# GDN entry of a hybrid decoder step on one NeuronCore: the first head's preparation interleaved with the decay chain, its weights divided by ScalarE and VectorE, the norm's high parts on ScalarE

## What is computed

```
h = x * rsqrt(mean(x*x) + eps) * w                # pre-norm, then
proj = h @ w_in                                   # GDN: q, k, v, z per head, and a, b (8 + 8 columns)
q, k, v = silu(causal_conv(qkv)); q, k = l2norm(q), l2norm(k)
beta = sigmoid(b);  g = -exp(A_log) * softplus(a + dt_bias);  G = cumsum(g) in each chunk
decay = exp(G_t - G_s);  M = I + strict_lower(beta * (k k^T) * decay)      # M is inverted by levels
A = (q k^T) * decay;  then the recurrence over chunks with M^-1, k, v and the state
```

## Time and profile before

| quantity | value |
|---|---|
| median of three runs | 1971.35 us |
| the profiled execution | 1978.76 us, its span 1976.5 us |
| TensorE busy | 92% of the span |
| VectorE / ScalarE / GpSimd busy | 57% / 27% / 25% |
| granted TensorE clock, mean | 0.951 |
| GDN entry, last tiles of U_AB to x2 of head 0 | 895 to 971.8 us of the span |

### The profile page before, as it was taken

One profiled execution on the slowest core, in us unless ns is written; L12 is line 12 of the kernel. 1 busy time (PEld: TensorE's weight loads), 2 busy tenths in 40 slices (PEclk: granted clock), 3 DMA queues, 4 the chain that ended last, 5 costly groups with the idle time before them and its releaser, 6 DMA issues.

```text
span 1976.5 us, 34445 instructions
## 1 busy us (share of the span) xinstructions
PE 1827.2 (92%) x13499; PEld 1743.0 (88%) x13499; DVE 1131.8 (57%) x1862; ACT 534.4 (27%) x981; POOL 499.1 (25%) x279
## 2 busy tenths in 40 slices
PE   3999999999999999997799999999989899999997
PEld 2888888888999999997788888888878799999996
DVE  5677777766625262676566666667653552525253
ACT  1444444443100000013243344344431300000011
POOL 1100000001556565662000000000000365655562
PEclk9989899989999999998798998999989899999997
DMA  5122222222232222331211211220112133222321
GB/s 173 46 63 67 63 68 73 65 76 78 75 86 86 86 85 86 92 77 45 55 35 36 65 47 30 56 67 21 45 52 69 51 90 86 86 85 85 88 82 45
DMA packets 257706, 136.76 MB, mean 69 GB/s; under 512 B 6730, under 2 KB 255908, under 8 KB 257636
## 3 DMA queue, kind: packets, MB, share of 16 engines
q1 hardware_dynamic: 219988, 115.08, 20.5%
q10 hardware_dynamic: 37648, 20.68, 3.6%
HBM read 123.75 MB, written 12.00 MB: 69 GB/s over the span
## 4 chain that ended last, share of the span: by engine, by line
PE 44%; DVE 5%; ACT 2%; issue 2%; DVEq 0%; ACTq 0%
PE pj L500 29%; PE rr L799 2%; PE rr L792 1%; PE rr L521 1%; PE rr L763 1%; PE rr L538 1%; DVE pr L1718 1%; PE rr L781 1%; PE rr L698 1%; PE rr L708 1%; DVE ol L1952 1%; DVE ws L1843 1%; PE rr L868 0%; PE rr L718 0%; PE rr L873 0%
## 5 line engine op out<-in xcount | busy, mean ns | idle before, releaser
L461 POOL TENSOR_SCALAR w_hi<-w_raw 128x1024 fp32r<-128x1024 f32 x137 | 145.2, 1060 | 1431.4 <-PE pj L500 1380.4
L500 PE MATMUL pj<-xh,w_hi 128*128 128x272 f32 x2064 | 468.1, 309 | 16.7 <-DVE xl L1452 7.7
L500 PE MATMUL pj<-xh,w_lo 128*128 128x272 f32 x2064 | 439.6, 295 | 0.0
L500 PE MATMUL pj<-xl,w_hi 128*128 128x272 f32 x2064 | 438.7, 295 | 0.0
L500 PEld LDWEIGHTS pj<-xh,w_hi 128*128 128x128 f32 x2064 | 335.5, 196 | 40.6 <-issue 19.8
L463 POOL TENSOR_TENSOR w_lo<-w_raw,w_hi 128x1024 fp32r<-128x1024 f32 x137 | 353.5, 2581 | 11.4
L500 PEld LDWEIGHTS pj<-xl,w_hi 128*128 128x128 f32 x2064 | 336.8, 196 | 0.0
L500 PEld LDWEIGHTS pj<-xh,w_lo 128*128 128x128 f32 x2064 | 335.9, 196 | 0.0
L500 PE MATMUL pj<-oh,w_hi 128*128 128x272 f32 x1248 | 264.9, 294 | 5.7 <-DVE w_lo L1497 3.1
L500 PE MATMUL pj<-oh,w_lo 128*128 128x272 f32 x1248 | 260.1, 290 | 0.0
L500 PE MATMUL pj<-ol,w_hi 128*128 128x272 f32 x1248 | 259.6, 290 | 0.0
(11 more groups left out here) (295 smaller groups left out, 2312.3 us busy)
## 6 DMA issues: line engine op xcount, KB each, us to landing
w_raw<-in_mlp_w_up_dram SPq DMA_DIRECT2D x64, 512.0 KB, 4.0
w_raw<-in_mlp_w_down_dram SPq DMA_DIRECT2D x64, 512.0 KB, 4.0
w_raw<-in_hgrn_w_in_dram SPq DMA_DIRECT2D x32, 512.0 KB, 4.1
w_raw<-in_gdn_w_in_dram SPq DMA_DIRECT2D x32, 512.0 KB, 4.2
out_dram<-S ACTq DMA_DIRECT2D x16, 512.0 KB, 3.4
w_raw<-in_hgrn_w_out_dram SPq DMA_DIRECT2D x9, 512.0 KB, 3.9
w_raw<-in_gdn_w_out_dram SPq DMA_DIRECT2D x9, 512.0 KB, 4.0
S<-in_state_hgrn_dram ACTq DMA_DIRECT2D x8, 512.0 KB, 4.1
```

Of the source, the lines that this page charges most:

```text
L461: nc.gpsimd.tensor_scalar(w_hi[:, s], w_raw[:, j], 1.0, 1.0, ALU.mult, ALU.mult).then_inc(hi_pool, 1)
L500: last = mm(pj[:, s, b, 0:HALF], w[:, s, k, :], v[:, k, b * HALF:(b + 1) * HALF], start=(k == 0 and a == 0), stop=(k == end - 1 and a == 2))
```

## The change

Four edits.

1. **The norm's high parts.** In n0 and n2 the product x*w into `xh` moves from VectorE (L1450) to ScalarE, an activation with the weight column as its scale, right after the square of the same k. VectorE's low part waits for it.
2. **Units 1 to 3 leave GpSimd.** `on_gpsimd` ends at U_GIN + 1. ScalarE's `high` of units 1, 2, 3 stands in `gdn_pre`; VectorE's `low` of 1 and 2 in `gdn_pre`, of 3 ahead of slot L3. `high` of 4 and 5 moves from behind the slots to behind L4 and L6, `low` of 4 and 5 to ahead of the evacuation of z and ahead of C0.
3. **Preparation inside the decay chain.** VectorE evacuates unit 0 and does slot L1 before the scan, and evacuates unit 1 at the end of the chain. The transposes of the history stand ahead of unit 0 on TensorE, and ScalarE does L1 and the first tap of k inside the chain. For head 0 the evacuations of v and z get places of their own (`evac2`, `evac3`). In all heads the copy `gnext` and the product `gsel` move from slot L1 to behind the convolution of k (L2). VectorE does `move` right behind `inverse`.
4. **All tiles of units 2 to 5 between the slots.** TensorE's counts are 4, 4, 6, 5, 5, 3, 2 ahead of L3, L4, L5, L6, C0, C2, C3, and 3 ahead of the first inverse: 32 tiles. Nothing stands between the first inverse and the recurrence.

```diff
 def on_gpsimd(u):
-    return u < 4 or U_MLP0 <= u < U_GIN + 4 or u >= U_MLP1
+    return u < 4 or U_MLP0 <= u < U_GIN + 1 or u >= U_MLP1
 # TensorE
 first_unit(U_AB, "n2")
-more = head_projections(U_GIN, 0)
-more(2 * KT)
+gdn_prepare("L1", 0)
+unit(U_GIN, 0, 0, xh, xl)
+unit(U_GIN, 0, 1, xh, xl)
 gdn_pre()
 pe.wait_ge(st["gp"][1].sem, st["gp"][1].after("cols", 0))
-for slot in GDN_SLOTS:
-    more(0 if slot == "L0" else 2)
+more = head_projections(U_GIN, 0, 2, 6)
+for slot, n in (("L3", 4), ("L4", 4), ("L5", 6), ("L6", 5), ("C0", 5), ("C2", 3), ("C3", 2)):
+    more(n)
     gdn_prepare(slot, 0)
+more(3)
 gdn_first_inverse(0, (st["ga"][1], "cout", 0))
-head_projections(U_GIN, 1, 0, 2)(2 * KT)
 # ScalarE, norm
     s.did(f(sq[:, k % 2], xT[:, k], ACT.Square), f"sq{k}")
+    if wcol is not None:
+        s.did(f(xh[:, k], xT[:, k], ACT.Copy, scale=vec[:, wcol + k:wcol + k + 1]), f"hi{k}")
 # ScalarE, gdn_pre
+high(0, U_GIN + 1)
+gdn_prepare("L1", 0)
 s.did(f(gsc[0:H, 2:3], gsc[0:H, 0:1], ACT.Exp), "A")
 ...
 s.did(f(gt4[32:64], B[32:64, 2], ACT.Exp), "be")
+high(0, U_GIN + 2)
+gdn_prepare("L2x", 0)
 ...
 s.did(f(gt4[96:96 + H], gt4[0:H], ACT.Exp), "eg")
+high(0, U_GIN + 3)
 sem_of(t, "cols", 0)
 # ScalarE, slots of head 0
+if slot == "L4":
+    high(0, U_GIN + 4)
+if slot == "L6":
+    high(0, U_GIN + 5)
 # VectorE, norm
-v.did(ts(xh[:, k], xT[:, k], w, None, ALU.mult), f"hi{k}")
-after(v, f"hi{k}", 0)
+after(s, f"hi{k}", 0)
 # VectorE, gdn_pre
 v.did(stt(... "neg")
+low(0, U_GIN + 1)
 ...
 v.did(ts(... "g2")
+gdn_prepare("evac0", 0)
+gdn_prepare("L1", 0)
 ...
 v.did(less_than_last(b[3][0:H], gt4[0:H]), "dl")
+low(0, U_GIN + 2)
+gdn_prepare("evac1", 0)
 # VectorE, slots of head 0
-for slot in GDN_SLOTS + ["inverse"]:
+for slot in ("L2", "L3", "L4", "evac2", "evac3", "L5", "L6", "C0", "C1", "C2", "C3", "inverse", "move"):
+    # low of unit 3 ahead of L3, of unit 4 ahead of evac3, of unit 5 ahead of C0
     gdn_prepare(slot, 0)
-low(0, U_GIN + 4)
-low(0, U_GIN + 5)
-gdn_prepare("move", 0)
```

More of the change, by code:

```diff
@@ L231, in build @@
             x=["copy"], xs=["copy"],
-            norm=[f"{n}{k}" for k in range(KT) for n in ("acc", "hi", "lo")], normf=[f"acc{k}" for k in range(KT)],
+            norm=[f"{n}{k}" for k in range(KT) for n in ("acc", "lo")], normf=[f"acc{k}" for k in range(KT)],
             normr=[f"lo{k}" for k in range(KT)],
@@ L239, in build @@
             gp=["x", "neg", "ls", "g", "g2", "scan", "dl"],
-            ga=["cols", "gsel", "k1", "k2", "k3", "kneg", "kls", "q1", "q2", "q3", "qneg", "dec", "ks", "qls", "kn", "kb",
+            ga=["cols", "k1", "k2", "k3", "kneg", "gsel", "kls", "q1", "q2", "q3", "qneg", "dec", "ks", "qls", "kn", "kb",
                 "v1", "v2", "v3", "vneg", "qs", "kkd", "vls", "vs", "qn", "zneg", "nl", "qkd", "zls", "tt0", "tt1", "A",
@@ L252, in build @@
             init=["lb1", "lb2", "lb3"],
-            norm=[f"sq{k}" for k in range(KT)] + ["ln", "rstd"], normf=[f"sq{k}" for k in range(KT)] + ["ln", "rstd"],
+            norm=[f"{n}{k}" for k in range(KT) for n in ("sq", "hi")] + ["ln", "rstd"], normf=[f"sq{k}" for k in range(KT)] + ["ln", "rstd"],
             normr=[f"{n}{k}" for k in range(KT) for n in ("sq", "hi")] + ["ln", "rstd"],
@@ L479, in _ @@
             run(U_MLP0, U_AB)
-            for u in range(U_AB, U_GIN + 4):
+            for u in range(U_AB, U_GIN + 1):
                 split(0, u)
@@ L977, in _, with norm @@
             s.did(f(lbt[:, 2], lbt[:, 0], ACT.Ln), "lb3")
-            def norm(key, u):
+            def norm(key, u, wcol=None):
                 v, s, t = st[key]
+                if wcol is not None:
+                    sem_of(st["init"][0], "vec", 0)
                 if u is None:
@@ L1338, in _ @@
             load_state(state_hgrn, 0)
-            norm("n0", None)
+            norm("n0", None, V_MIX)
             for slot in range(3, 10):
@@ L1349, in _ @@
             mlp("up0")
-            norm("n2", U_AB - KT)
+            norm("n2", U_AB - KT, V_MIX + KT)
             gdn_pre()
             for slot in GDN_SLOTS:
-                gdn_prepare(slot, 0)
-            high(0, U_GIN + 4)
-            high(0, U_GIN + 5)
+                if slot not in ("L1", "L2x"):
+                    gdn_prepare(slot, 0)
+                if slot == "L4":
+                    high(0, U_GIN + 4)
+                if slot == "L6":
+                    high(0, U_GIN + 5)
             gdn_first_inverse(0)
@@ L1735, in decayed @@
                     v.did(tt(dst[0:TS, TP:T], rr[0:TS, bank, 2 * P:2 * P + TS], dec[0:TS, TP:T], ALU.mult), name)
-                if slot == "L0":
+                ahead = isinstance(h, int) and h == 0
+                if slot in ("L0", "evac0"):
                     evacuate(0, 0)
+                if slot in ("L0", "evac1"):
                     evacuate(1, 1)
+                if slot == "evac2":
+                    evacuate(2, 0)
+                if slot == "evac3":
+                    tt(halves(pr[:, 2, 0:T]), computed(U_GIN, h * 4, 3), halves(rstd[:]), ALU.mult).then_inc(unit_out, 1)
                 if slot == "L1":
-                    cp(hc[:, 4:5], cf[:, ds(h + C_HSEL, 1)])
                     cp(hcw[:], cw[:].rearrange("p j (g x) -> p j g x", g=3)[:, :, :, ds(h, 1)]
                        .rearrange("p j g o -> p j (g o)"))
-                    v.did(cp(gnext[:], of_head(0).rearrange("p c o -> p (c o)")), "cols")
+                    v.did(cp(hc[:, 4:5], cf[:, ds(h + C_HSEL, 1)]), "cols")
+                if slot == "L2":
+                    convolve("k", "ktap", 0, K_ROW)
+                    cp(gnext[:], of_head(0).rearrange("p c o -> p (c o)"))
                     after(v, "cols", h)
                     v.did(ts(work, gt4[:], hc[:, 4:5], None, ALU.mult), "gsel")
-                if slot == "L2":
-                    convolve("k", "ktap", 0, K_ROW)
                 if slot == "L3":
@@ L1761, in gdn_prepare @@
                     v.did(log_sigmoid(1, YW), "qls")
-                    evacuate(2, 0)
+                    if not ahead:
+                        evacuate(2, 0)
                 if slot == "L5":
@@ L1780, in gdn_prepare @@
                     v.did(stt(out=nQ, in0=nQ, scalar=float(P) ** -0.5, in1=G, op0=ALU.mult, op1=ALU.mult), "qn")
-                    tt(halves(pr[:, 2, 0:T]), computed(U_GIN, h * 4, 3), halves(rstd[:]), ALU.mult).then_inc(unit_out, 1)
+                    if not ahead:
+                        tt(halves(pr[:, 2, 0:T]), computed(U_GIN, h * 4, 3), halves(rstd[:]), ALU.mult).then_inc(unit_out, 1)
                     dve.wait_ge(unit_out, h * 4 + (U_GIN + 3 + 3))
@@ L1986, in _ @@
             after(st["gp"][1], "cols", 0)
-            for slot in GDN_SLOTS + ["inverse"]:
+            for slot in ("L2", "L3", "L4", "evac2", "evac3", "L5", "L6", "C0", "C1", "C2", "C3", "inverse", "move"):
+                if slot == "L3":
+                    low(0, U_GIN + 3)
+                if slot == "evac3":
+                    low(0, U_GIN + 4)
+                if slot == "C0":
+                    low(0, U_GIN + 5)
                 gdn_prepare(slot, 0)
-            low(0, U_GIN + 4)
-            low(0, U_GIN + 5)
-            gdn_prepare("move", 0)
             low(0, U_GIN + 6)
```

## The result

The changed kernel took 1960.62 us (median of 15 runs, 1953.16 to 1970.71), the kernel before beside it 1970.04 (15 runs, 1966.0 to 1979.02): ratio 0.9936, interval 0.9917 to 0.9956. That is 12.6 us faster by the ratio, where 28.6 were forecast. The profiled execution took 1967.13, its span 1965.1. One execution of the kernel before (2279.6 us) and one of e1_gsel_back (3461.89 us) fell into a slower state and stand outside all ratios.

What follows compares the result with a forecast made beforehand. TensorE's work plus its holes was taken as the bound, with VectorE waiting for GpSimd second. Entry 25.1 (n2 included) plus n0 3.5 gave 28.6 us: 1971.35 to 1942.7, said as 1943; range 1937 to 1956.

Steps and rivals of the forecast that it cites:

- The entry: GDN entry up to dt2 of head 0: preparation and TensorE units lie beside each other, dt2 25.1 us earlier.
- n2's 0.65: Norm n2: the low part of k = 6 and k = 7 end sooner, so U_AB ends 0.65 us earlier.
- The lock: VectorE waits for whole GpSimd instructions over a shared port pair; five stretched decay-chain rows lose this, together 8.0 us.
- part 1: Decay chain: with units 1 to 3 off GpSimd, five VectorE rows of 1.53 to 2.66 us fall to 0.2 to 0.7.
- the reading by which only TENSOR_SCALARs are held: Norm n2, alternative: xl 6 would be there at 890.5 and U_AB would end 1.5 us earlier.
- n0, 3.5 us: Norm n0: without the high part on VectorE the sum starts 3.5 us earlier; bounds 1.5 and 5.5.
- A: GDN entry: the clock stays low, six units cost 6.9 us more, gain 21.7, time 1949.7; chance 0.25 together with B.
- B: Entry's slots: weight halves standing in them cost 7 us, gain 21.6, time 1949.7; chance 0.25 together with A.
- The step that failed: Loop over heads and tiles from unit 6 onwards: taken as unchanged, with weights early; no cost put in the sum.
- Rival D: Recurrence: a denser start lowers its clock; at 0.86 the loss is 37.7 us and the time 1980; chance 0.03.

Runs made afterwards that it cites:

- e1_gsel_back: The changed kernel with gnext and gsel back in slot L1, for head 0 ahead of the convolution of k; run twice: 0.9861 and 0.9836 of before.
- e5: The kernel before with only gnext and gsel moved behind the convolution of k: 1.0063 of before, 12.4 us slower.
- e3: The changed kernel with the norms' high parts on VectorE again: 0.9953 of before.
- e0_after: The changed kernel run again, nothing altered: 0.9921 of before.
- e7_units_behind: e1_gsel_back with units 4 and 5 behind the first inverse and their halves behind the slots: 0.9896 of before.

## Why the prediction was wrong

- *The entry, 25.1 us earlier at dt2 (n2's 0.65 in it)*: right in kind, a little high. From rstd to dt2 it was 77.9 us before and is 55.2 after, 22.7 less, where 24.5 were forecast. cols came 13.2 us after rstd (said: some 13), x2 48.8 (said: 49). What fails is behind x2: from there to dt2 it was 6.3 us, where the forecast had 4.35. I had TensorE wait 1.8 us for the low part of unit 6. It waited 2.34 and for something queued behind it, the evacuation of unit 4, which frees the PSUM slot. The two tiles and dt2 then ran at the lower level (12 matmul records in 2.74 us where before they took 1.70; dt2 1.60).
- *The lock*: all five rows fell to 0.17 to 0.71 us, as worked out in part 1. In n2 xl 6 has two SBUF inputs and took 2.91 us instead of 0.78; it ended 0.6 us behind GpSimd's low part (890.22 + 2.91 = 893.13, 889.81 + 2.74 = 892.55). That agrees with the rule of the Trainium skill ("SBUF — State Buffer", "SBUF: two separate sides") and rules out the reading by which only TENSOR_SCALARs are held. From rstd of n1 to that of n2 it was 389.8 us and is 389.3: 0.5, where 0.65 were forecast.
```profile
890.22 2.91 DVE L1465 SCALAR_TENSOR_TENSOR xl<-xT,vec,xh 128x544 fp32r<-128x544 f32 x1
...
889.81 2.74 POOL L463 TENSOR_TENSOR w_lo<-w_raw,w_hi 128x1024 fp32r<-128x1024 f32 x1
```
- *n0, 3.5 us*: mis-sized, 5.2 measured, near the upper bound of 5.5, which stood for the case in which VectorE alone sets the pace. It did at the end: TensorE waited for xl there, 0.27 and 0.32 us. The sum starts 4.2 us earlier, and the other 1 us is its own duration, 1.08 instead of 2.02, which I had left out.
- *Rivals A and B*: the granted clock was 1.00 up to 945, so A did not happen. From cols to the inverse's first level VectorE took 32.7 us, as forecast, so B did not either. (The "hole of 23.5 us" under A is the length of a stretch with 9.70 us of TensorE in it, so 13.8 us of idle time.)
- **The step that failed** is the sentence "The tiles of unit 6 onwards and the loop over heads are unchanged". The section on the change says that gnext and gsel move in all heads; I priced them once, at 0.6 us in head 0, and did not ask who waits behind them in the loop. There VectorE's next instruction is sr1, and TensorE's L799 waits for it. The term was put at nothing. Its direct price is 0.5 us a head, 3.5 in all; the measured one is 12.4 us alone (e5) and the difference between the changed kernel (0.9921 to 0.9936) and e1 (0.9836 to 0.9861), 12 to 20 us.
- *Does the sum close?* The parts that I forecast do, by the traces: 22.7 + 0.5 + 5.2 = 28.4 of 28.6. Without the term e1 is 27 to 32 us faster than before, but its two intervals reach from 19 to 40, and the agreement is in part luck: beside the trace of before, e1's has the rest of head 0 behind dt2 4.0 us longer and heads 1 to 5 9.6 us shorter, which no term of the forecast has.
- *Rival D* had the right stretch and the right resource, the clock of the recurrence, and the wrong reason. I argued "the loop's own instructions are what sets its density, and they don't change". The instructions didn't change, but their order did.
- *The scatter*: I did not ask how far single executions scatter. Within the 15 runs of the changed kernel the time follows the mean granted clock: 1953.16 at 0.959, 1970.71 at 0.948, a fitted 0.36 us for each us at the lower level.

## What to carry to other kernels

When a diff moves an instruction in a helper that the loop uses too, price it once per trip, and name the instruction behind it and the engine that waits for that. In this kernel, with TensorE 94 to 95% busy in the loop, half a microsecond of delay a trip cost 1.8 us on the average (12.4 over 7 trips), so look at the granted clock of one trip beside its length before and after. Judge a change of under 1% on such a kernel by many runs, not by two traces: HGRN's 450 us were 442 and 456 in two executions of one program.

## What was unexpected of the hardware

- The heads settle in a pattern. In e1 four heads in turn take 68.2 us with 6.8 us at the lower level, in e3 four take 71.6 to 71.7 with 13.7; after and e0_after repeat 68.5, 70.6, 72.1, 71.8, 68.8 to 0.1 us in different executions. So in these two executions the program set the pattern, while HGRN's time differed between them (456.4 and 442.2).
- In the heads of e1 and after shown above TensorE counts as busy for 94 to 95% and no wait in heads 1 to 5 is above 2.0 us, and still its clock falls in each head. The Trainium skill, page "TensorE: Matmul & The Clock Gate", section "HAM oscillation — how this bites in real kernels", names gaps in TensorE's work as what lets the clock fall. These traces show no simple form of that: head for head, idle time and granted clock don't go together. TensorE is idle for 3.2 us at a clock of 0.95 (e1's head above), 4.3 at 0.91 (after's), 4.7 at 0.97 (e7_units_behind) and 5.2 at 0.93 (e5_gsel_only). What in a head sets its clock stays open. The heads of e7 and e5:
```profile
1093.15:1161.37 68.22, 63.50 (x479) 58.56 (x478) 46.69 (x107) 29.82 (x66) 0.00 (x0) 0.97 0.18 48
1106.18:1178.03 71.85, 66.62 (x479) 61.38 (x478) 46.73 (x106) 30.18 (x66) 0.00 (x0) 0.93 0.18 47
```
